# Part of VectorE's work in three norms and in the second attention given to GpSimd

## The reference

```
# first block, layer l (mod: shifts, scales and gates from a condition vector)
h  = mod(rms_norm(x, g_pre_mix));  y = [MLA | short conv | SSD](h @ w_in) @ w_out
x  = x + gate1 * rms_norm(y, g_post_mix)
h  = mod(rms_norm(x, g_pre_ffn));  f = relu(h @ w_ff1)**2 @ w_ff2
x  = x + gate2 * rms_norm(f, g_post_ffn)
# second block: layer 0 has mixer_a (three dilated windows), layer 1 mixer_b
s  = q k^T * scale, masked to a band; m = max(s, sink); e = exp(s - m)
o  = (e @ v) / (sum(e) + exp(sink - m))          # mixer_b; mixer_a is without sinks
x  = layer_norm(alpha * x + (o * silu(z)) @ w_out);  x += sigmoid(x @ w_gate) * (p @ w_proj)
```

## Time and profile before

| | |
|---|---|
| median of 3 runs | 1689.22 us (1688.07 to 1692.46) |
| profiled execution | 1697.89 us, its span 1696.1 us |
| TensorE matmuls busy | 1564.8 us, 92% of the span |
| VectorE busy | 984.4 us, 58% |
| ScalarE busy | 918.0 us, 54% |
| GpSimd busy | 63.3 us, 4%, 82 instructions |
| DMA | 225.40 MB, mean 133 GB/s |

### The profile page before, as it was taken

How to read it: one execution, slowest core, us unless ns; L and a number is a source line. 1 busy time by engine, 2 the same in 40 slices (tenths; PEclk the granted TensorE clock), 3 DMA queues, 4 the chain that set the end, 5 groups by cost and what they waited for, 6 DMA issues and landing times.

```text
span 1696.1 us, 25703 instructions
## 1 busy us (share of the span) xinstructions
PE 1564.8 (92%) x10227; PEld 1315.7 (78%) x10227; DVE 984.4 (58%) x1602; ACT 918.0 (54%) x1518; POOL 63.3 (4%) x82
## 2 busy tenths in 40 slices
PE   5999898979999999979989989998999999888887
PEld 3777555748788888848845889998999999888777
DVE  2463666564343434464754676667766767577655
ACT  5653645464132323455555554556777867376745
POOL 3000032000000000000003000000000000000000
PEclk9999977989999999989986899999999999999899
DMA  7731535342433232342306366663635444343232
GB/s 245 222 99 50 174 100 174 119 129 75 149 100 99 91 102 82 113 143 75 124 13 207 118 197 191 197 199 128 227 127 173 150 150 141 109 133 117 91 108 75
DMA packets 223640, 225.40 MB, mean 133 GB/s; under 512 B 8234, under 2 KB 222064, under 8 KB 223472
## 3 DMA queue, kind: packets, MB, share of 16 engines
q1 hardware_dynamic: 222816, 223.63, 41.1%
q0 software_dynamic: 704, 0.12, 0.0%
HBM read 222.68 MB, written 1.05 MB: 132 GB/s over the span
## 4 chain that ended last, share of the span: by engine, by line
PE 73%; ACT 11%; DVE 11%; issue 2%; POOL 1%; DMA 0%; SPq 0%; DVEq 0%; ACTq 0%; POOLq 0%
PE bank L1039 20%; PE bank L1040 19%; PE bank L1041 19%; ACT SH L1701 2%; PE bank L1075 2%; ACT whi L1565 1%; DVE wlo L2116 1%; PE bank L1327 1%; PE bank L1060 1%; ACT H L1807 1%; PE bank L1234 1%; ACT HH L1807 1%; PE bank L1242 1%; PE bank L1349 1%; PE bank L1394 1%
## 5 line engine op out<-in xcount | busy, mean ns | idle before, releaser
L2116 DVE TENSOR_TENSOR wlo<-raw,whi 128x1024 fp32r<-128x1024 f32 (+2 forms) x322 | 387.9, 1208 | 259.0 <-ACT whi L1565 254.5
L1565 ACT ACTIVATE whi<-raw 128x1024 fp32r<-128x1024 f32 (+2 forms) x322 | 336.0, 1046 | 278.7 <-PE bank L1041 259.1
L1039 PE MATMUL bank<-HH,whi 128*128 128x512 f32 (+2 forms) x640 | 246.2, 385 | 22.1 <-DVE HL L2138 19.3
L1040 PE MATMUL bank<-HL,whi 128*128 128x512 f32 (+2 forms) x640 | 241.9, 378 | 0.0
L1041 PE MATMUL bank<-HH,wlo 128*128 128x512 f32 (+2 forms) x640 | 241.7, 378 | 0.0
L1039 PE MATMUL bank<-HA,whi 128*128 128x256 f32 x576 | 165.4, 287 | 13.7 <-DVE LA L2138 5.2
L1040 PE MATMUL bank<-LA,whi 128*128 128x256 f32 x576 | 162.3, 282 | 0.0
L1041 PE MATMUL bank<-HA,wlo 128*128 128x256 f32 x576 | 162.1, 281 | 0.0
L1039 PEld LDWEIGHTS bank<-HH,whi 128*128 128x128 f32 (+1 forms) x640 | 121.3, 190 | 50.8 <-issue 17.0
L1041 PEld LDWEIGHTS bank<-HH,wlo 128*128 128x128 f32 (+1 forms) x640 | 121.0, 189 | 23.6 <-issue 0.7
L1040 PEld LDWEIGHTS bank<-HL,whi 128*128 128x128 f32 (+1 forms) x640 | 121.5, 190 | 22.9 <-issue 1.2
(11 more groups left out here) (371 smaller groups left out, 3208.1 us busy)
## 6 DMA issues: line engine op xcount, KB each, us to landing
raw<-in_w_ff_dram SPq DMA_DIRECT2D x64, 1024.0 KB, 5.3
raw<-in_w_mod_dram SPq DMA_DIRECT2D x48, 1024.0 KB, 5.2
raw<-in_a_w_in_dram SPq DMA_DIRECT2D x40, 1024.0 KB, 5.0
raw<-in_w_in_dram SPq DMA_DIRECT2D x18, 1024.0 KB, 5.3
raw<-in_b_w_in_dram SPq DMA_DIRECT2D x9, 1024.0 KB, 5.3
raw<-in_w_out_dram SPq DMA_DIRECT2D x8, 1024.0 KB, 5.2
raw<-in_ple_w_gate_dram SPq DMA_DIRECT2D x8, 1024.0 KB, 5.1
raw<-in_a_w_out_dram SPq DMA_DIRECT2D x4, 1024.0 KB, 5.0
```

Source lines behind the costliest of these rows:

```text
L1039: nc.tensor.matmul(o, wh, xh, start=start, stop=False, skip_group_check=shared)
L1040: nc.tensor.matmul(o, wh, xl, start=False, stop=False, skip_group_check=shared)
L1565: f(whi[h % HALF_SLOTS][:, 0:n], raw[u.id % RAW_SLOTS][:, (h % 2) * n:(h % 2) * n + n], ACT.Copy)\
L2116: v.tensor_tensor(wlo[h % HALF_SLOTS][:, 0:n], raw[u.id % RAW_SLOTS][:, (h % 2) * n:(h % 2) * n + n], whi[h % HALF_SLOTS][:, 0:n].bitcast( ...
```

## The change

In the second attention VectorE stops at the reciprocal, and GpSimd multiplies the exponentials by it. In the norms (0, mix), (0, ffn) and (1, mix) GpSimd updates tiles 3 and 7 of `XT`, VectorE the other six, each by itself instead of in pairs; (1, ffn) stays as it was. Readers of the two tiles wait on GpSimd's signal. The clearing of the pads, which waited for tile 7, waits for tile 6.

```diff
@@ TensorE, att2_turn
-            pe.wait_ge(s_p2, s_p2.at(ip))
+            if i == 0:
+                pe.wait_ge(s_p2, s_p2.at(ip))
+            else:
+                pe.wait_ge(s_p2_pool, s_p2_pool.at(ip))
@@ ScalarE, norm_sum
-                    act.wait_ge(s_x_new, s_x_new.at((l, "mix", k) if which == "ffn" else (l - 1, "ffn", k)))
+                    at_ = (l, "mix", k) if which == "ffn" else (l - 1, "ffn", k)
+                    if k in X_POOL:
+                        act.wait_ge(s_x_pool, s_x_pool.at(at_))
+                    else:
+                        act.wait_ge(s_x_new, s_x_new.at(at_))
@@ VectorE, norm
+                if (l, which) != (0, "mix"):
+                    for k in X_POOL:
+                        dve.wait_ge(s_x_pool, s_x_pool.at((l, "mix", k) if which == "ffn" else (l - 1, "ffn", k)))
@@ VectorE, post
-            for a_, b_ in ((0, 2), (2, 4), (4, 6), (6, 7), (7, 8)):
+            last = (l, which) == (LAYERS - 1, "ffn")
+            for a_, b_ in ((0, 2), (2, 4), (4, 6), (6, 7), (7, 8)) if last else ((0, 1), (1, 2), (2, 3), (4, 5), (5, 6), (6, 7)):
@@ VectorE, att2_scale
             if i == 1:
                 chain(v.tensor_tensor(small[:, total:total + 4], small[:, total:total + 4], small[:, sink:sink + 4], ALU.add))
+                v.reciprocal(small[:, inv:inv + 4], small[:, total:total + 4]).then_inc(*s_p_inv.tick(ip))
+                return
@@ GpSimd   (X_POOL = (3, 7))
-                        pool.wait_ge(s_x_new, s_x_new.at((l - 1, "ffn", KC - 1)))
+                        pool.wait_ge(s_x_new, s_x_new.at((l - 1, "ffn", KC - 2)))
...
+            elif kind == "att2_second" and args[0][0] == 1:
+                ip = args[0]
+                pool.wait_ge(s_p_inv, s_p_inv.at(ip))
+                for e in (0, 1):
+                    for part, (a, n) in enumerate(((0, P), (P, SEQ))):
+                        c = att_col(ip, 3, e, part)
+                        p_ = att_p(ip, e)[:, a:a + n]
+                        ins = nc.gpsimd.tensor_tensor(p_, p_, bc(small[:, c:c + 1], [P, n]), ALU.mult)
+                ins.then_inc(*s_p2_pool.tick(ip))
+            elif kind == "post" and args != (LAYERS - 1, "ffn"):
+                l, which = args
+                t = t_of(l)
+                sl = slice(t[0], t[1])
+                pool.wait_ge(s_inv, s_inv.at(("p", l, which)))
+                for n, k in enumerate(X_POOL):
+                    if n > 0:
+                        pool.wait_ge(s_x_pool, s_x_pool.at((l, which, X_POOL[n - 1])))
+                    pool.wait_ge(s_yg, s_yg.at((l, which, k)))
+                    x = XN[k // 2 % 2][:, k % 2, sl]
+                    nc.gpsimd.tensor_tensor(x, YM[:, k, sl], RS[:, sl], ALU.mult).then_inc(*s_xg.tick((l, which, k)))
+                    pool.wait_ge(s_xg, s_xg.at((l, which, k)))
+                    nc.gpsimd.tensor_tensor(XT[:, k, sl], XT[:, k, sl], x, ALU.add).then_inc(*s_x_pool.tick((l, which, k)))
```

More of the change, by code:

```diff
@@ L261, in build @@
     s_p2 = signal("p2")
+    s_p_inv = signal("p_inv")
+    s_p2_pool = signal("p2_pool")
     s_p_hi = signal("p_hi")
@@ L310, in build @@
     s_x_new = signal("x_new")
+    s_x_pool = signal("x_pool")
+    s_xg = signal("xg")
     s_xc = signal("xc")
@@ L847, in build @@
     last_win = {u.key[0]: u.id for u in units if u.kind == "win"}
+    X_POOL = (3, 7)
     mla_last = {l: (l, MLA_HEADS - 1, 1) for l in range(LAYERS)}
```

## The result

The changed kernel takes 1701.01 us in the median (11 runs, 1697.26 to 1702.06), the kernel before 1692.46 in the 11 runs beside it (1688.07 to 1696.97). The ratio is 1.0049, 95% interval 1.0036 to 1.0063: slower by some 8.3 us. The forecast was 1692.2 us and its range ended at 1697.5; the measured time lies 8.8 above the forecast and 3.5 above the range. Of the 8.8 us, 3.3 are not the change's: the forecast stood on a median of 3 runs of the kernel before, 1689.22, and its 11 runs gave 1692.46. The other 5.5 are the medians' difference, 8.5 where +3.0 was forecast. The profiled execution took 1702.02 us, its span 1700.0.

A forecast was written before the change was run, and what follows sets the result against it. TensorE, 92% busy, was taken as the bound, so norm losses or gains arrive in full at the end. Norms +6.0 and attention -3.0 gave +3.0 on a median of 1689.22: 1692.2 us, range 1683.5 to 1697.5.

The forecast's parts named there:

- The forecast's case: Whole kernel: within 0.3% of before, norms lose and the attention gives back about half, +3.0 us; chance 0.48.
- slower: Rival, chance 0.30: the attention's relief is spent in ScalarE's own queue, the norms stand alone, +6.0 us, 1695.2.
- with the clock at half in the norms, +9: Clause in the slower rival and upper bound of the norms: TensorE's clock falls in wider gaps between tile sums; 1698.
- Two engines on one port: Norms: VectorE and GpSimd take turns on SBUF, 1.69 us a 512-column pair, so each GpSimd instruction costs VectorE 1.03.
- The rival by which GpSimd holds VectorE for its whole instruction: Norms: VectorE pays 1.26 and 0.72 us for each GpSimd instruction, 2.8 more, 1695.0; chance 0.05 of the slower 0.30.
- Splitting costs nothing: Norms: pairs of tiles become single ones on VectorE; the forecast added no separate cost for this.
- The norms at full clock, +2.1, +2.5, +1.4: Delay of the refinement in norms 0/mix, 0/ffn and 1/mix, in us, from VectorE sharing turns with GpSimd.
- the norms' term, +6.0: The three norms' delays together, +6.0 us, bounds +3 and +9; the weight split follows ScalarE's square of the sixth tile.
- The attention, -3.0: Second attention: GpSimd's scaling lets VectorE and ScalarE run earlier, -3.0 us, bounds 0 and -5.
- the waits of 1.02 and 1.36 us: Second attention: TensorE's waits for the maxima and the gated product would shrink to nothing, 2.4 us.
- the +0.3 of the forecast: Second attention, pair 1: VectorE arrives 1.0 us earlier, GpSimd scales in 2.4, so the scaling ends 0.3 later.
- The sum: Norms +6.0 and attention -3.0 us give +3.0 for the whole kernel, 1692.2 us.

The follow-up runs named there:

- e4: e1 with GpSimd's four instructions per norm turned into clearings that read nothing, tiles 3 and 7 not updated; 1686.3 us, 0.9966 of the kernel before.
- e3: The kernel before with all eight tiles of the three norms updated singly on VectorE, none on GpSimd, attention as before; 1692.3 us, ratio 0.9998.
- e5: The changed kernel with idle matmuls ahead of the first three tile sums of the two wide norms; 1695.5 us, 1.003 of the kernel before.
- e12: e1 with idle matmuls in the two wide norms, second attention as before; 1696.5 us, 1.0015 of the kernel before.
- e1: The change's norms alone, the second attention as in the kernel before; 1702.9 us, 1.006 of the kernel before.
- e2: The change's second attention alone, the norms as in the kernel before; 1689.5 us, 0.999 of the kernel before.
- e7: The change's norms with only tile 7 on GpSimd, seven tiles singly on VectorE, attention as before; 1697.9 us, 1.004 of the kernel before.

## Why the prediction was wrong

*The forecast's case* (0.48, +3.0 us) did not come; the case "slower" (0.30) did, but by the clause that stood in its price, "with the clock at half in the norms, +9", and not by its mechanism, a relief spent in ScalarE's queue.

- **Two engines on one port:** right. 1.68 us for a pair of instructions against 1.69, 1.64 and 1.75 against "about 1.7". VectorE's 12.1 us for its six tiles are exact. The rival by which GpSimd holds VectorE for its whole instruction would give 0.66 + 1.26 = 1.92 a pair and is refuted. That is also the rule of the Trainium skill (SBUF — State Buffer, Who interferes with whom), that the later one is blocked until the first has finished; the trace has 0.24 us less for each pair, and the measurement decides. e4 shows that GpSimd's presence, its signals and its writes don't hold VectorE; what is left is its reading of SBUF, or its arithmetic, which no run separates from it.
- **Splitting costs nothing:** right in the time (e3, 0.9998), with ways 0.4 to 0.8 us longer.
- **The norms at full clock, +2.1, +2.5, +1.4:** right in the trace. The forecast's ways are 15.8, 15.8 and 9.5; e5 has 15.81, 15.81 and 9.48. In time it is less sure: e12, which has these ways and the attention of before, came out at +0.3 to +4.7 us, and only the figure at equal clock (+5.6) is near 6.0.
- **The failed step is the size of the norms' term, +6.0,** where it goes from the sixth tile to the weight split with "ScalarE squares it" and nothing else. That takes TensorE's sums to be out of the way. The sixth tile is out 10.8 us behind the first multiply in (0, mix), as forecast; what comes behind it is not. In the trace a tile's sum at half clock takes 2.05 us, ScalarE's squares wait up to 1.70 for it, and the split comes 12.0 and 13.2 us behind the first multiply instead of 11.4. The term measured 8.4 us in the ways instead of 6.0, and 1.006, 10 us, in e1. The clock stood in the text as the bound of +9 and its row was quoted; the forecast took the value without it, although the same passage saw wider gaps between the tile sums and a half clock in the kernel before. That filling the gaps takes 2.3 of the 8.4 us away again (e5) shows the clock as their cause. From the split to the refinement it is 4.36 us in both wide norms (362.72 to 367.08, 750.36 to 754.72), as forecast.
- **The attention, -3.0:** the direction right, the size too large. e2 has -1.7 at equal clock, the change against e1 -2.8 ± 1.5, e5 against e12 -1.9 ± 1.2; about -2. The forecast let the waits of 1.02 and 1.36 us shrink to nothing, 2.4 together; in e2 they shrink by 1.02 and 0.46, and the wait of 3.08 stays. At pair 1 the +0.3 of the forecast came, by luck, from parts that were off: VectorE comes to it 0.6 earlier and not 1.0 (8.56 us from pair 0's reciprocal to pair 1's, 9.17 before), because it saves the 1.01 of the scaling but loses 0.45 in the two-column instructions behind the maxima, which take 0.81 instead of 0.36 while GpSimd scales. GpSimd takes 1.90 for a pair and not 2.4. The turn then comes 1.95 us behind the scaling's start (1565.72 to 1567.67) where it came 1.13 behind it; together 10.84 us behind pair 0's reciprocal, where it was 10.52. VectorE's wait for ScalarE's split ahead of it is as long as before (1.06, and 1.08 in the row below), since ScalarE itself comes earlier by as much.

The row of VectorE in the kernel before, ahead of pair 1:

```profile
1556.49 2.36 DVE L2116 TENSOR_TENSOR wlo<-raw,whi 128x1024 fp32r<-128x1024 f32 x2 [1.08 <-ACT whi L1565]
```

- **The sum.** At equal clock the change costs +3.5 ± 0.9 us; the forecast's sum was +3.0. The other 4.5 of the 8.0 us between the means are the clock, 0.9490 for 0.9549. Such a difference is 2 x 0.0059 x 1700 = 20 us at half clock, and the windows of the two wide norms hold 6.7 + 9.8 - 3.4 = 13 of them.

**Left open:** where the other 7 us at half clock lie, and why they come. The ways account for 2.3 us (8.4 less e5's 6.1) of the clock's 4.5. One place where such time comes and goes can be named. Up to the second attention e2 and the kernel before are the same program, and in their profiles all matmuls up to 900 us start within 0.25 us of each other. Then e2 reaches the first multiply of norm (1, mix) at 966.37 and the kernel before at 972.94, 6.6 us later. The windows over this part of the SSD, first before and then e2:

```profile
850.00:950.00 100.00, 85.16 (x463) 56.37 (x462) 55.60 (x121) 50.18 (x114) 17.84 (x22) 0.73 0.29 95
```

```profile
850.00:944.00 94.00, 77.00 (x468) 50.90 (x467) 55.87 (x121) 49.87 (x114) 18.52 (x22) 0.84 0.32 101
```

So one program's SSD part differs by 6.6 us between two runs, half of the spread of its runs, and its clock with it. The changed kernel's profile has the same 0.73 there (858 to 958 us) as that of the kernel before; the 4.0 us at the end of their comparison hold none of it. Whether the changed kernel's timed runs meet the slow SSD more often than those of the kernel before isn't shown. That clock lost in the norms costs by the fitted rate was not tried by itself.

## What to carry to other kernels

Work given to GpSimd isn't free for VectorE when both have two inputs in SBUF at the same time: here a helper that starts at the same moment delays the head of a chain by more than it takes off its tail; half as much work for it (e7) halves the loss at equal clock and doesn't turn it. Where a change stretches a gap between short matmuls, look at the granted clock there and price those matmuls at half, in the sum and not as a bound. And where runs spread more than the effect, set each run's time against its granted clock before an average is believed.

## What the runs showed of the hardware

- VectorE and GpSimd, both with two inputs in SBUF, take turns at 1.68 us for a pair of 512 columns (0.66 and 1.26 alone) and 0.87 for 256 (979.97 to 981.71 is two pairs); beside GpSimd's clearings, which take 0.53, VectorE keeps its 0.69.
- Even VectorE instructions of two columns, 0.36 us for two of them (1552.50, with GpSimd idle), took 0.81 beside GpSimd's 128- and 256-column multiplies (1558.40 and 1566.97). The maxima ahead of them, with one input in a bank of TensorE's results, kept their 0.29 and 0.42 us beside the same multiplies.
- 14 idle matmuls of 128 columns in a norm (28 in the trace's count) kept TensorE's clock at 2.4 GHz through gaps in which it had fallen to 1.2; they delayed none of the sums: the ways became shorter, 17.59 to 15.81 us.
- 0.01 of mean granted clock went with 7.6 us of 1700 in this kernel, and accounts for most of the spread of its runs (correlation within kernels -0.86). In the SSD part alone it differed between 0.73 and 0.84 for the same program, and 6.6 us went with it.
